# Expert up product with the weights as stationary operand, and expert weights loaded with neighbouring rows per partition

## The reference

```
h = rmsnorm(x) * norm_ffn_w                         # (tokens, 1024)
g = argmax(h @ w_rc); fine = (h @ w_rf)[group g]    # router, 4 + 32 columns
two largest of softmax(fine), weights normalised
for each expert e of 32:
    hu   = h @ w_eu[e]                              # 1024 -> 512
    act  = silu(hu[:, :256]) * hu[:, 256:]
    out += combine_weight * (act @ w_ed[e])         # 256 -> 1024
```

## Time and profile before

| | us |
|---|---|
| median of 3 runs | 1746.57 (1742.38 to 1747.7) |
| the profiled execution | 1747.29 |
| its span in the profile | 1745.5 |

### The profile page before, as it was taken

One profiled execution on the slowest core, in us unless ns is written; L12 is line 12 of the kernel. 1 busy time (PEld: TensorE's weight loads), 2 busy tenths in 40 slices (PEclk: granted clock), 3 DMA queues, 4 the chain that ended last, 5 costly groups with the idle time before them and its releaser, 6 DMA issues. The chain is left out here.

```text
span 1745.5 us, 15906 instructions
## 1 busy us (share of the span) xinstructions
PE 1513.9 (87%) x5982; PEld 939.8 (54%) x5982; DVE 700.6 (40%) x1088; ACT 410.8 (24%) x675; POOL 213.7 (12%) x222
## 2 busy tenths in 40 slices
PE   3999999989988989599999599999807999999960
PEld 3666666645655656356989366555403444444430
DVE  3595087522344322785785333221241111111118
ACT  6211200115474564231211500011101111111113
POOL 0000000000000000254287000000041000000004
PEclk9999999999999999799899899999958999999995
DMA  5136028521101112424101722211128999999947
GB/s 155 51 87 112 25 74 259 124 77 40 38 25 26 34 31 78 101 61 137 58 1 29 296 75 75 61 62 62 43 72 305 378 366 371 374 369 365 367 139 275
DMA packets 191316, 247.83 MB, mean 142 GB/s; under 512 B 62548, under 2 KB 125432, under 8 KB 190976
## 3 DMA queue, kind: packets, MB, share of 16 engines
q1 hardware_dynamic: 165608, 186.82, 33.9%
q10 hardware_dynamic: 18040, 34.45, 5.1%
q0 software_dynamic: 7584, 25.44, 3.9%
HBM read 188.86 MB, written 57.82 MB: 141 GB/s over the span
## 5 line engine op out<-in xcount | busy, mean ns | idle before, releaser
L651 PE MATMUL P<-arena 128*128 128x352 f32 (+1 forms) x1776 | 557.3, 470 | 0.0
L651 PEld LDWEIGHTS P<-arena 128*128 128x128 f32 (+1 forms) x1776 | 336.9, 193 | 191.7 <-issue 29.5
L1056 PE MATMUL P<-arena 128*128 128x512 f32 x512 | 227.9, 598 | 0.8 <-ACT arena L2026 0.8
L1056 PEld LDWEIGHTS P<-arena 128*128 128x128 f32 x512 | 95.9, 192 | 110.0 <-issue 110.0
L1004 PE MATMUL P<-arena 128*128 128x512 f32 (+1 forms) x288 | 126.8, 595 | 1.9 <-DVEq L1489 1.9
L972 PE MATMUL P<-arena 128*128 128x352 f32 x384 | 115.9, 465 | 9.3 <-DVE arena L1475 9.3
L1043 PE MATMUL P<-arena 128*128 128x512 f32 x256 | 115.3, 593 | 0.9 <-DVE arena L1618 0.9
L1598 DVE COPY arena<-P 128x512 f32<-128x512 f32 x32 | 22.1, 692 | 213.8 <-PE P L1030 213.8
L972 PEld LDWEIGHTS P<-arena 128*128 128x128 f32 x384 | 74.0, 193 | 51.8 <-issue 12.1
L1004 PEld LDWEIGHTS P<-arena 128*128 128x128 f32 (+1 forms) x288 | 50.9, 181 | 66.7 <-issue 64.2
L576 POOL TENSOR_TENSOR arena<-arena,N 64x256 f32<-64x256 f32 x96 | 79.9, 832 | 48.2 <-ACT arena L1960 26.9
(11 more groups left out here) (383 smaller groups left out, 1832.7 us busy)
## 6 DMA issues: line engine op xcount, KB each, us to landing
arena<-in_w_expert_up_dram SPq DMA_DIRECT2D x32, 2048.0 KB, 12.2
arena<-in_w_expert_down_dram SPq DMA_DIRECT2D x32, 1024.0 KB, 7.6
arena<-in_w_in_dram SPq DMA_DIRECT2D x36, 512.0 KB, 3.9
y_d<-arena ACTq DMA_DIRECT2D x32, 512.0 KB, 7.5
gate_d<-arena ACTq DMA_DIRECT2D x16, 528.0 KB, 4.2
arena<-gate_d SPq DMA_DIRECT2D x16, 528.0 KB, 4.5
arena<-in_x_prompt_dram SPq DMA_DIRECT2D x16, 512.0 KB, 4.1
y_d<-zero SPq DMA_DIRECT2D x1, 8192.0 KB, 34.8
```

The lines of the kernel that those rows point to most:

```text
L651: m = pe.matmul(P[0:p, b + j, 0:TBK], w[:, k, 0:p], hT[:, k, TBK * j:TBK * j + TBK], start=f, stop=l)
L1056: m = pe.matmul(P[:, i % 2, :], xgT[i % 2][:, k, :], WU[i % NWE][:, k, :], start=k == 0, stop=k == KD - 1)
```

## The change

Two things are changed together.

**The up product is turned round.** Each 128x128 block of `WU` is stationary and the 128 tokens of `xgT[:, k, :]` move past it. The output is features x tokens: four groups f of 128 features, each accumulated over eight k into 128 columns of the same PSUM bank. That is 32 products with 128 moving columns in place of 8 with 512. Groups 0 and 1 are gate features, 2 and 3 up features. Because the result already has the features on partitions, the product of gate and up is written straight to `hactT`; the two transposes, the copy, the buffers `hact` and the semaphore `s_hat` are gone. `down(i)` waits for `s_ha` instead, and DVE's multiply waits for `s_dn`.

**Expert weights are loaded as "(p k) f -> p k f"**: partition p holds rows 8p to 8p+7 of `w_eu[e]` (16 KB in one piece) and rows 2p and 2p+1 of `w_ed[e]` (8 KB in one piece). To match, `h2` is written with its columns permuted, so that block k holds features k, 8+k, 16+k and so on; the router weights are loaded the same way. For the down product the feature block k on partition p must be feature 2p+k, so the stationary operand of group f takes every second column of `WU`: columns 256*(f//2) + f%2, then in steps of 2.

```diff
@@ PE
             def down(i):
-                pe.wait_ge(s_hat, i + 1)
+                pe.wait_ge(s_ha, i + 1)
...
-                    for k in range(KD):
-                        m = pe.matmul(P[:, i % 2, :], xgT[i % 2][:, k, :], WU[i % NWE][:, k, :], start=k == 0,
-                                      stop=k == KD - 1)
+                    for f in range(4):
+                        for k in range(KD):
+                            first = FF * (f // 2) + f % 2
+                            m = pe.matmul(P[:, i % 2, 128 * f:128 * f + 128], WU[i % NWE][:, k, first:first + 255:2],
+                                          xgT[i % 2][:, k, :], start=k == 0, stop=k == KD - 1)
                     m.then_inc(s_up, 1)
                     if i + 1 < hi:
                         gathered(i + 1)
                     if i > lo:
                         down(i - 1)
-                    pe.wait_ge(s_ha, i + 1)
-                    bank = bank6()
-                    for k in range(2):
-                        m = pe.transpose(bank[:, 128 * k:128 * k + 128], hact[i % 2][:, 128 * k:128 * k + 128], ident)
-                    m.then_inc(s_6, 1)
@@ DVE
+            by_k = lambda v: v.rearrange("t (p k) -> t k p", k=KD)
...
-                dve.scalar_tensor_tensor(h2[i % 2][0:n, :], x1[0:n, i, :], st[0:n, a + 3:a + 4], WB[0:n, :], ALU.mult,
-                                         ALU.mult).then_inc(s_h2, 1)
+                dve.scalar_tensor_tensor(h2[i % 2][0:n, :].rearrange("t (k p) -> t k p", k=KD), by_k(x1[0:n, i, :]),
+                                         st[0:n, a + 3:a + 4], by_k(WB[0:n, :]), ALU.mult, ALU.mult).then_inc(s_h2, 1)
...
-                    dve.tensor_tensor(hact[i % 2], gact[i % 2], P[:, i % 2, FF:2 * FF], ALU.mult).then_inc(s_ha, 1)
+                    if i >= 2:
+                        dve.wait_ge(s_dn, i - 1)
+                    dve.tensor_tensor(hactT[i % 2], gact[i % 2], P[:, i % 2, FF:2 * FF].rearrange("p (a b) -> p a b", a=2),
+                                      ALU.mult).then_inc(s_ha, 1)
                     if i > lo:
                         down(i - 1)
-                    bk = bank6()
-                    dve.tensor_copy(hactT[i % 2].rearrange("p a b -> p (a b)"), bk[:, 0:2 * 128]).then_inc(s_hat, 1)
-                    dve.wait_ge(s_hat, i + 1)
-                    dve.sem_inc(s_6f, 1)
@@ ACT
-                    act.activation(gact[i % 2], P[:, i % 2, 0:FF], ACT.Silu).then_inc(s_ga, 1)
+                    act.activation(gact[i % 2], P[:, i % 2, 0:FF].rearrange("p (a b) -> p a b", a=2), ACT.Silu).then_inc(s_ga, 1)
@@ SP: w_rc, w_rf, w_eu[0, e], w_ed[0, e]
-                sp.dma_start(WU[b], w_eu[0, e].rearrange("(k p) f -> p k f", p=128)).then_inc(s_w[b], 16)
+                sp.dma_start(WU[b], w_eu[0, e].rearrange("(p k) f -> p k f", p=128)).then_inc(s_w[b], 16)
```

More of the change, by code:

```diff
@@ L251, in hybrid_step @@
         yo = [at(q2 + 4096 + i * D, D) for i in range(2)]
[L252 to L255, removed]
+        gact = [at(q2 + 6144 + i * FF, 2, 128) for i in range(2)]
+        hactT = [at(q2 + 6656 + i * FF, 2, 128) for i in range(2)]
+        assert q2 + 7168 <= q
         JF = at(2 * TT_ * D, D)
@@ L422, in hybrid_step @@
         s_wf = sem("s_wf")
-        s_hat = sem("s_hat")
         s_xgT6 = sem("s_xgT6")
@@ L2261, in _ @@
                     sp.dma_start(WB, norm_ffn.broadcast_to([128, D])).then_inc(s_wb, 16)
-                    sp.dma_start(WRr[:, :, 0:NG], w_rc[0].rearrange("(k p) n -> p k n", p=128)).then_inc(s_wb, 16)
-                    sp.dma_start(WRr[:, :, NG:NG + E], w_rf[0].rearrange("(k p) n -> p k n", p=128)).then_inc(s_wb, 16)
+                    sp.dma_start(WRr[:, :, 0:NG], w_rc[0].rearrange("(p k) n -> p k n", p=128)).then_inc(s_wb, 16)
+                    sp.dma_start(WRr[:, :, NG:NG + E], w_rf[0].rearrange("(p k) n -> p k n", p=128)).then_inc(s_wb, 16)
                 if i >= 1:
@@ L2277, in expert @@
                 e = sp.value_load(te_i[0:1, i:i + 1], min_val=0, max_val=E - 1)
-                sp.dma_start(WU[b], w_eu[0, e].rearrange("(k p) f -> p k f", p=128)).then_inc(s_w[b], 16)
+                sp.dma_start(WU[b], w_eu[0, e].rearrange("(p k) f -> p k f", p=128)).then_inc(s_w[b], 16)
                 if i >= NWE:
                     sp.wait_ge(s_dn, i - NWE + 1)
-                sp.dma_start(WD[b], w_ed[0, e].rearrange("(k p) f -> p k f", p=128)).then_inc(s_wd[b], 16)
+                sp.dma_start(WD[b], w_ed[0, e].rearrange("(p k) f -> p k f", p=128)).then_inc(s_wd[b], 16)
             sp.wait_ge(s_te, 1)
```

## The result

The changed kernel takes 1762.09 us (median of 4 runs, 1761.45 to 1763.66) against 1745.36 us for the kernel before (4 runs, 1742.38 to 1747.70). The ratio is 1.0089, 95% interval 1.0073 to 1.0106: slower by 0.9%, some 15.5 us. The profiled execution took 1761.45 us, its span is 1759.7 us, 14.2 more than before.

A forecast was written before the change was run, and what follows sets the result against it. PE was taken as the bound, with DMA keeping up. +9.5 (up product) - 6.5 - 0.5 - 1.3 (transposes) + 0.7 (h2) gave +1.9 us: 1749.2 profiled, 1748.5 as median; range 1738 to 1772, the forecast's own 1742 to 1754.

The forecast's parts named there:

- rival (b): Up product's weight loads: strided loads are slower; small penalty +18 us, 1765, chance 0.12; large +125, 1872 us, chance 0.05.
- my own sign: Trace after: up product 7.17 us per tile; wrong if under 6.95 or over 7.3, or PE waits between tiles.
- The other sign named for rival (b): Trace after: if loads pay for their step, their mean length rises above the delta stage's, at any DMA load.
- What bounds the kernel: Expert stage: PE is the bound, DMA keeps up; one tile costs 11.40 us, 32 times.
- The form of the pass: Up product: 64 passes of 128 columns with own loads, 0.112 us each, 7.17 us, +0.30 per tile, +9.5 in all.
- The stationary operand's step: Up product's weight loads: reading every second float, 8 bytes apart, costs 0; upper end 0.172 us per load.
- Transposes: Activation transposes go: 0.22 us of PE in 30 tiles, -6.5 us; first tile -0.5, last tile -1.3.
- The permuted h2: DVE's h2 operation: 0.7 us longer, hidden in eight of nine row tiles, +0.7 us on the path in the last.
- Transfers: Expert weight loads in larger pieces: no gain as no matmul waited for weights; cost on the gather taken as 0.
- rival (c): Expert stage: gather late behind 16 KB pieces, deciding at 9.3 us; at 10.5 us +36, about 1784 us; chance 0.07.
- Instructions: Expert stage: feeding PE about 80 matmuls and 80 loads in 11.5 us, beside full DMA, costs 0.

The follow-up runs named there:

- both kernels with contiguous blocks: Changed kernel with 128 neighbouring columns per stationary block and old down-weight layout, 1749.56 us, ratio 0.9996; and the same with all old layouts, 1750.26 us, ratio 0.9997.
- the kernel with the up product alone: Changed kernel with contiguous stationary blocks and expert weights, h2 and router weights in their old layouts: 1750.26 us, ratio 0.9997 to the kernel before.
- layout-alone kernel: Kernel before with the new weight loads and permuted h2, its activation transposes taking every second column: 1748.83 us, ratio 0.9993.
- contiguous kernel with 64 moving columns: Changed kernel with contiguous stationary blocks and old down-weight layout, multiplying only the first 64 of each tile's 128 tokens: 1758.42 us, one profiled run.

## Why the prediction was half right

I forecast 1748.5 us, no measurable change; 1762.09 came, inside the range, as the small form of rival (b). But by my own sign the forecast's mechanism was wrong: I had said that I was wrong if the up piece is over 7.3 us, and it is 7.53. The other sign named for rival (b) is there too: the loads last longer, 196 ns at the median where contiguous ones last 192.

- **What bounds the kernel: right.** PE without idle time in the stage, before and after. All that changed in the stage is PE's own time.
- **The form of the pass: right.** 0.112 us from the earlier trace rows; 0.1116 in both kernels with contiguous blocks. The ratio of four short passes to a long one is 4 x 0.1116/0.429 = 1.04, as I read it.
- **The stationary operand's step: this step failed.** I took 0, "since 8 bytes are far nearer to none than to 128". It is 0.1177 - 0.1116 = 0.0061 us per pass, 64 x 32 x 0.0061 = +12.5 us. The miss on the profiled executions is 1761.5 - 1749.2 = 12.3 us. That the two agree so well is in part chance: the contiguous pass, 0.1116 in place of 0.112, takes 0.9 us off, and 0.9 us comes from outside the stage (below). Nearness in bytes was the wrong yardstick. What counts is how many 16-byte lines a load opens against a load that is already the bound of its pass. The rows could have warned me: the earlier trace rows show the load alone at 0.106 of a pass of 0.112, so that a slower load comes through. The upper end, 0.172, was not far-fetched either: it is the price of a step of 3.
- **Rival (b)** decided, at a pitch of 0.1177 where it starts at 0.114 and I had priced 0.120 with 1765 us. I gave it 0.12; its mechanism was right.
- **Transposes: right.** They are gone, -0.22 us a tile. At tile 1 the transposes of the tokens start 1335.67 - 1333.85 = 1.82 us before up(1), in place of 2.23: -0.4 where I had -0.5. In the last tile down(31) follows down(30) at once, the two take 1705.46 - 1698.41 = 7.05 us by the chain in place of 8.43: -1.4 where I had -1.3.
- **The permuted h2: right.** 2.06 us where I had 2.0, and on the path in the last row tile alone: PE's wait for the copy behind it went from 4.08 to 4.87 us. From that tile's addition (L1505) to the first operation of the routing (L1521) it is 13.12 us, 12.33 with the old form in the kernel with the up product alone, so +0.8 where I had +0.7.
- **Transfers: right in the outcome, wrong in the slack.** No wait for a weight and none for a gather, though the worst gathers took 9.6 and 10.8 us, over the 9.3 where rival (c) was to decide. That point was wrong: I had taken the transposes after the gather's issue for the ones that need it, and they are one turn later, so that it decides at some 21 us. The 0.07 for rival (c) and its +36 us rested on that.
- **Instructions: right.** 281 matmuls in 40 us beside a DMA share of 0.97, with no idle time.

The stage, from the start of up(0) to the end of the last down product, went from 369.1 to 381.7 us: +12.6. By the terms it is 0.66 x 32 - 6.5 - 0.5 - 1.3 = +12.8. The rest of the span's +14.2 lies outside it. up(0) starts 3.9 us later: 3.4 us are there before the last h2 operation, 2.7 of them from 900 to 1000 us, in work that the change does not touch; 0.8 is h2; 0.9 is the router's product behind it, 3.60 us in place of 2.69, all of it at the lower clock; and the routing is 1.2 us shorter. The end of the kernel is 2.3 us shorter, where the last `y_d` store landed in 3.4 in place of 5.5 us. Apart from h2 I take these for differences between runs; they were not tested. The kernel with the up product alone, whose h2 is the old one, has the 3.60 us too.

## What to carry to other kernels

When a product is turned round so that the large operand becomes stationary, the weight loads are no longer covered by long passes, and what slows a load is paid times the number of passes: here a step of 2 cost 0.006 us, 2048 times. Count the 16-byte lines that a float32 load opens: keep the stationary blocks contiguous, and choose the permutation of features in the weights' own layout so that they are; here the new layout earned nothing while PE was the bound. And two harmless edits can be harmful together: price the pair, not the parts.

## What the runs showed of the hardware

- A 128x128 float32 load costs, within 2% of what was measured, the larger of its own time, 0.111 us at the upper clock and 0.217 at the lower, and some 1.81 ns for each 16-byte line opened: 0.1116, 0.1177, 0.1739, 0.2314 and 0.2358 us per pass for steps of 1, 2, 3, 4 and 8 floats. I had not expected a step of 8 to cost as little as one of 4, nor 128 and 64 moving columns to cost the same (7.14 and 7.09 us).
- The activation transposes with every second column took 0.23 in place of 0.22 us for two in the layout-alone kernel. As far as two decimals tell, that is the same 5% per pass; with two passes per tile it comes to nothing.
- In the contiguous kernel with 64 moving columns the granted clock stayed at 0.50 through the first two up products and the transposes behind each, though PE was busy 13.87 of 13.90 us, and rose at 1353.0 us, just after the first down product had begun (1352.83). In the changed kernel it rose within the first up product (10.29 us at a mean of 0.73) and was 1.00 in the second (7.78 us).
- A 3 MB load issued while small scatters run on another queue made the read behind them 4.8 us later.
